# A two-layer diffusion backbone: one store form for the turned heads, query loads in 2 KB runs, rows of maxima from two queues, softmax sums in four column tiles

## The reference

```
z = h @ w_in; q_a, kv_a, k_rope, gq, gk, gv = split(z)
q  = (rms_norm(q_a, g_q_a) @ w_q_b)     # 8 heads of 64 + 32 (the 32 are rotated)
kv = (rms_norm(kv_a, g_kv_a) @ w_kv_b)  # 8 heads: 64 of key, 64 of value
gq, gk = rms_norm per head, rotated     # 8 query heads, 2 key heads of 64
o = concat(softmax(q_mla @ k_mla * scale) @ v_mla, softmax(gq @ gk * scale) @ gv)
x = layer_norm(ALPHA * x + gate * (o @ w_o)); then a two-level mixture of 32 experts
```

## Time and profile before

| | |
|---|---|
| median of 3 runs | 3547.01 us (3544.86 to 3549.27) |
| the profiled execution's own time | 3557.03 us |
| its span, first to last instruction | 3555.3 us |
| mean granted TensorE clock | 0.952 |
| TensorE matmul busy | 3211.8 us, 90% |
| VectorE busy | 2629.5 us, 74% |
| ScalarE busy | 1783.9 us, 50% |
| GpSimd busy | 1399.5 us, 39% |
| attention of layer 0 | about 385 to 940 us of the span |
| attention of layer 1 | about 2145 to 2659 us of the span |

### The profile page before, as it was taken

One profiled execution on the slowest core, in us unless ns is written; L12 is line 12 of the kernel. 1 busy time (PEld: TensorE's weight loads), 2 busy tenths in 40 slices (PEclk: granted clock), 3 DMA queues, 4 the chain that ended last, 5 costly groups with the idle time before them and its releaser, 6 DMA issues. The chain is left out here.

```text
span 3555.3 us, 44667 instructions
## 1 busy us (share of the span) xinstructions
PE 3211.8 (90%) x14764; PEld 2296.7 (65%) x14764; DVE 2629.5 (74%) x2481; ACT 1783.9 (50%) x2050; POOL 1399.5 (39%) x1103
## 2 busy tenths in 40 slices
PE   6999599998896999999959986999989699999995
PEld 3777455544484788888847764555447578888882
DVE  2444466677687899999967765777868799999995
ACT  2333233333410788888844432333432188888883
POOL 2111011121211777777732210111112278888882
PEclk9999699999997999999979997999999799999997
DMA  7665722221253989779953536222216489899965
GB/s 271 246 237 188 203 62 66 68 63 51 102 217 157 335 313 380 286 290 385 347 199 126 175 123 183 73 54 54 63 34 229 188 298 378 304 371 347 333 236 209
DMA packets 285993, 732.61 MB, mean 206 GB/s; under 512 B 65265, under 2 KB 174353, under 8 KB 234537
## 3 DMA queue, kind: packets, MB, share of 16 engines
q0 software_dynamic: 111056, 502.86, 38.3%
q1 hardware_dynamic: 157368, 175.09, 16.0%
q10 hardware_dynamic: 17440, 53.10, 4.1%
HBM read 723.65 MB, written 122.40 MB: 238 GB/s over the span
## 5 line engine op out<-in xcount | busy, mean ns | idle before, releaser
L2260 DVE TENSOR_TENSOR ex_wl<-ex_back,ex_wh 128x2048 fp32r<-128x2048 f32 x288 | 652.8, 2293 | 94.0 <-ACT ex_wh L2174 94.0
L1300 ACT ACTIVATE at_pt<-at_st 128x1024 f32<-128x1024 f32 (+1 forms) x336 | 336.6, 1004 | 561.9 <-PE at_st L1235 560.8
L2174 ACT ACTIVATE ex_wh<-ex_back 128x2048 fp32r<-128x2048 f32 x288 | 551.4, 1920 | 30.5 <-PE ex_vp L2105 17.2
L1353 DVE TENSOR_REDUCE at_nm<-at_sc 128x1 f32<-128x1280 f32 (+1 forms) x276 | 378.4, 1371 | 218.8 <-PE at_sc L1200 216.0
L1367 DVE TENSOR_TENSOR at_acc<-at_acc,at_pt 128x1024 f32<-128x1024 f32 x256 | 321.7, 1257 | 95.4 <-ACT at_pt L1300 93.2
L2260 DVE TENSOR_TENSOR ex_wl<-ex_front,ex_wh 128x2048 fp32r<-128x2048 f32 x144 | 324.0, 2290 | 12.5 <-ACT ex_wh L2174 12.1
L1249 PE MATMUL at_op<-at_pt,at_va 128*64 128x512 f32 (+1 forms) x1344 | 321.3, 607 | 0.2
L2174 ACT ACTIVATE ex_wh<-ex_front 128x2048 fp32r<-128x2048 f32 x144 | 275.3, 1923 | 86.2 <-SPq L2051 60.7
L2011 POOL DMA_INDIRECT ex_back<-in_w_down,piece_of x144 | 282.2, 1960 | 48.0 <-issue 43.4
L1235 PE MATMUL at_st<-at_q,at_km 96*128 96x512 f32 (+3 forms) x1008 | 267.2, 406 | 16.9 <-DMA at_q<-at_nmT 14.9
L1235 PEld LDWEIGHTS at_st<-at_q,at_km 96*128 96x128 f32 (+1 forms) x1008 | 181.4, 194 | 104.5 <-issue 53.6
(11 more groups left out here) (298 smaller groups left out, 6797.1 us busy)
## 6 DMA issues: line engine op xcount, KB each, us to landing
ad_w<-in_w_ada POOLq DMA_DIRECT2D x48, 1024.0 KB
at_q<-q_g SPq DMA_DIRECT2D x48, 256.0 KB, 4.4
k_n<-T SPq DMA_DIRECT2D x20, 512.0 KB, 3.6
q_n<-T SPq DMA_DIRECT2D x20, 512.0 KB, 4.2
q_g<-T SPq DMA_DIRECT2D x20, 512.0 KB, 3.4
at_km<-k_n SPq DMA_DIRECT2D x16, 640.0 KB, 10.5
mr_ot<-o_s SPq DMA_DIRECT2D x18, 512.0 KB, 5.5
h_s<-mr_h ACTq DMA_DIRECT2D x18, 512.0 KB, 2.7
```

The source lines that it names most:

```text
L1300: nc.scalar.activation(pt[:, j % PT, :, 0:nq], st[:, j % 2, :, 0:nq], ACT.Exp).then_inc(exp_done, 1)
L1353: nc.vector.tensor_reduce(nm[:, v % 3, s:s + 1], score_bank(A_NO[v, s])[:, 0:kb * P], AX.X, ALU.max, negate=True).then_inc(max_done, 1)
L2174: nc.scalar.activation(wh[:, q], early.raw(u, p), ACT.Copy).then_inc(hi_done, 1)
L2260: nc.vector.tensor_tensor(wl[:, q], early.raw(u, p), wh[:, q].bitcast(F32), ALU.subtract).then_inc(lo_done, 1)
```

## The change

1. The four groups of turned heads are stored in one form, `heads0` to `heads3`, each `[128, 2, 4, 1280]`: all in 512-byte runs, one store a group. Five stores a tile instead of eight.
2. Queries are loaded from there with the tokens of up to four tiles in one run of 2 KB (1 KB for a context unit) instead of 512 bytes, and lie in `q` by head, then tile. Keys are loaded as before, from the new names.
3. SP sends the rows of maxima of one head; the rows of the other are sent by ScalarE's queue, right behind the copy that made them.
4. The sums over partitions are four products of 32 columns of ones and half as many queries, except for the last unit, instead of two of 64 columns. ScalarE's copy is half as long, and one DMA instead of two sends the sums to memory.

```
-        NST = 8
+        NST = 5
...
-            def put_k(t):
-                sp.dma_start(S["k_n"][:, :, :, bass.ds(t * P, P)], T[0][:, :, :, :].bitcast(F32)).then_inc(q_stored, 16)
-
-            def put_q(t):
-                sp.dma_start(S["q_n"][bass.ds(t, 1)].rearrange("a p x h n -> p (a x) h n"), T[1][:, :, :, :].bitcast(F32)).then_inc(q_stored, 16)
...
+            def put(t, g):
+                sp.dma_start(S[f"heads{g}"][:, :, :, bass.ds(t * P, P)].rearrange("p x j n -> p (x j) n"),
+                             T[g][:, :, :, :].rearrange("p x j n -> p (x j) n").bitcast(F32)).then_inc(q_stored, 16)
...
-        q = sb("q", [P, QR, 2, 4, 2, P], F32R)
+        q = sb("q", [P, QR, 2, 2, 4, P], F32R)
...
-            eng.dma_start(dst.bitcast(F32), src.rearrange("a (h d) n -> d a h n", h=2)).then_inc(q_loaded[s][x], 16)
+            eng.dma_start(dst[:, :, 0:na, :].rearrange("p h a n -> p h (a n)").bitcast(F32),
+                          src.rearrange("(h d) n -> d h n", h=2)).then_inc(q_loaded[s][x], 16)
...
+        def set_row(eng, v, h):
+            pair, t0, na, kb, nq = place(v)
+            at, x = (QK, 0) if pair < G0 else (HD, 1)
+            eng.wait_ge(nm_out, T_NO[v] + 1)
+            for a in range(na):
+                eng.dma_start(q[at:at + 1, v % QR, x, h, a, :].bitcast(F32),
+                              nmT[2 * a + h:2 * a + h + 1, T_NO[v] % 2, :].bitcast(F32)).then_inc(row_set[v % QR], 16)
...
-                for h in range(2):
-                    ins = nc.tensor.matmul(op[VD * h:VD * h + VD, 0:nq], C["ones"][:, 0:VD], acc[:, u % 2, h, 0:nq], start=True, stop=True)
+                if u == len(U) - 1:
+                    for h in range(2):
+                        ins = nc.tensor.matmul(op[VD * h:VD * h + VD, 0:nq], C["ones"][:, 0:VD], acc[:, u % 2, h, 0:nq], start=True, stop=True)
+                else:
+                    for part in range(4):
+                        ins = nc.tensor.matmul(op[QB * part:QB * part + QB, 0:nq // 2], C["ones"][:, 0:QB],
+                                               acc[:, u % 2, part // 2, (part % 2) * nq // 2:(part % 2 + 1) * nq // 2], start=True, stop=True)
...
                 nc.scalar.activation(nmT[0:2 * na, n % 2, :], sc[0:2 * na, 1280:1408], ACT.Copy).then_inc(nm_out, 1)
+                set_row(act, v, 1)
...
-                for h in range(2):
-                    pool.dma_start(S["den_s"][s:s + 1, h * nq:(h + 1) * nq], den[VD * h:VD * h + 1, s, 0:nq]).then_inc(den_kept, 16)
-                pool.wait_ge(den_kept, 32 * (u + 1))
+                pool.dma_start(S["den_s"][s, 0:2 * nq].rearrange("(j n) -> j n", j=4),
+                               den[0:3 * QB + 1:QB, s, 0:nq // 2]).then_inc(den_kept, 16)
+                pool.wait_ge(den_kept, 16 * (u + 1))
```

More of the change, by code:

```diff
@@ L313, in _ @@
                 load_rope(t)
[L314 to L317, removed]
+                for g in range(4):
+                    put(t - 1, g)
                 put_v(t - 1)
@@ L327, in _ @@
             put_v(t)
[L328 to L335, removed]
+            for g in range(4):
+                sp.wait_ge(lo_done, 4 * t + g + 2)
+                put(t, g)
             sp.wait_ge(q_stored, 16 * NST * NT + 1)
@@ L977, in attention @@
     PT, QR, RC = 8, 5, 32
+    QB = P // 4
     SC = [(0, 512), (512, 1024), (1024, 1280)]
@@ L1104, in load_q @@
                     return
-                src, dst = S["q_g"][t0:t0 + na, :, part, pair - G0, :], q[part * HD:(part + 1) * HD, s, x, 0:na]
-            eng.dma_start(dst.bitcast(F32), src.rearrange("a (h d) n -> d a h n", h=2)).then_inc(q_loaded[s][x], 16)
+                src, dst = S["heads3"][:, part, pair - G0, tokens], q[part * HD:(part + 1) * HD, s, x]
+            eng.dma_start(dst[:, :, 0:na, :].rearrange("p h a n -> p h (a n)").bitcast(F32),
+                          src.rearrange("(h d) n -> d h n", h=2)).then_inc(q_loaded[s][x], 16)
         def load_k(eng, pair, x, part):
             if part == 0:
-                src, dst = S["k_n"][:, x, pair, :].rearrange("(h d) n -> d h n", h=2), km[0:NOPE, pair % 2, x]
+                src, dst = S["heads0"][:, x, pair, :].rearrange("(h d) n -> d h n", h=2), km[0:NOPE, pair % 2, x]
             else:
-                src, dst = S["k_r"][:, x, :].unsqueeze(1).to_broadcast([ROPE, 2, NT * P]), km[NOPE:QK, pair % 2, x]
+                src, dst = S["heads2"][0:ROPE, x, 3, :].unsqueeze(1).to_broadcast([ROPE, 2, NT * P]), km[NOPE:QK, pair % 2, x]
             eng.dma_start(dst.bitcast(F32), src).then_inc(k_loaded[pair % 2][x], 16)
+        def set_row(eng, v, h):
[5 more added lines that the diff above has]
+                              nmT[2 * a + h:2 * a + h + 1, T_NO[v] % 2, :].bitcast(F32)).then_inc(row_set[v % QR], 16)
         @block.sync
         def _(sp):
[L1118 to L1124, removed]
             def store(u):
@@ L1138, in _ @@
             for v in early:
-                set_row(v)
+                set_row(sp, v, 0)
             for x in range(2):
@@ L1228, in scores @@
                         K = km[:, pair % 2, :, h, keys]
-                        passes = [(K[0:QK + 1, 0], q[0:QK + 1, s, 0, 0:na, h, :]), (K[0:QK, 0], q[0:QK, s, 1, 0:na, h, :]),
-                                  (K[0:QK, 1], q[0:QK, s, 0, 0:na, h, :])]
+                        passes = [(K[0:QK + 1, 0], q[0:QK + 1, s, 0, h, 0:na, :]), (K[0:QK, 0], q[0:QK, s, 1, h, 0:na, :]),
+                                  (K[0:QK, 1], q[0:QK, s, 0, h, 0:na, :])]
                     else:
                         kv = (pair - G0) // 2
-                        passes = [(kg[:, kv, keys], q[:, s, 0, 0:na, h, :]), (kl[0:HD + 1, kv, keys], q[0:HD + 1, s, 1, 0:na, h, :])]
+                        passes = [(kg[:, kv, keys], q[:, s, 0, h, 0:na, :]), (kl[0:HD + 1, kv, keys], q[0:HD + 1, s, 1, h, 0:na, :])]
                     for m, (kk, qq) in enumerate(passes):
@@ L1403, in _ @@
             pool.dma_start(va[:, :, :], S["v_s"].rearrange("(t p) n -> p t n", p=P)).then_inc(v_loaded, 16)
-            gk = [S["k_g"][:, x, :].rearrange("(h d) n -> d h n", h=H_KV) for x in range(2)]
+            gk = [S["heads2"][:, x, 2, :].rearrange("(h d) n -> d h n", h=H_KV) for x in range(2)]
             for half in range(2):
@@ L2475, in backbone @@
     dram("ada", [2, DEPTH * 6 * D])
[L2476 to L2481, removed]
+    for g in range(4):
+        dram(f"heads{g}", [P, 2, 4, NT * P])
     dram("v_s", [NT * P, (H_MLA + H_KV) * VD])
```

24 lines of the change are left out of this document (9 added, 15 removed).

## The result

The changed kernel takes 3567.06 us (median of 7 runs, 3561.65 to 3583.01), the kernel before 3547.47 (7 runs, 3543.06 to 3550.39). The ratio is 1.0062, 95% interval 1.0044 to 1.0080: 22 us slower, 16 to 28 by the interval. The forecast was 3538.8 within 3523 to 3557, with 0.17 on slower. The profiled execution took 3567.06, its span is 3565.3 and its clock 0.948.

A forecast was written before the change was run, and what follows sets the result against it. Attention was taken as bound by TensorE, in GQA units only just. Terms -14 +12.8 -4.6 -5.0 +2.8 -1.0 -2.4 +3.2 gave -8.2 us, 3538.8 us for the median, range 3523 to 3557.

The forecast's parts named there:

- Rows issued by ScalarE: Unit hand-overs: ScalarE's four DMAs, 0.59 us each, delay the exponential and then VectorE's maximum; +12.8 us, bounds 0 and +22.
- In MLA units ... the delay is covered.: MLA hand-overs: scores take longer, TensorE comes later for the maximum, so no cost; without that cover 0.75 us each.
- 0.75 for each of 11 such hand-overs.: GQA hand-overs: TensorE loses 0.6 to 0.7 us, the next maximum can add 0.35; taken as 8.3 us in all.
- The rival that names this place: Slower: ScalarE's issuing, from 0.7 us an issue or a falling clock, holds up GQA units; +11, 3558 us; chance 0.17.
- The clock: GQA units: the slower hand-over gives TensorE two more stretches at lower clock; +3.2 us, bounds 0 and +16.
- Waits for rows: Units of layer 0: SP's last row leaves 2.5 us sooner, ending TensorE's waits; -4.6 us, bounds 0 and -5.4.
- The starts: Both starts of attention: two queues issue the last row 2.5 us earlier; -5.0 us for both layers, bounds 0 and -12.5.
- The sums: Sums in four column tiles: a latent unit takes TensorE 0.52 us for 1.00; -14 us, bounds -15.2 and -10.
- The inverse: Layer 0: one DMA instead of two brings sums forward 0.8 us at three waits; -2.4 us, bounds 0 and -8.
- Stores of one form: End of projections: 512-byte runs store slower, delaying attention's first load 1.4 us a layer; +2.8 us, bounds -4 and +4.5.
- Inside the loop the same wait is covered by TensorE's products: Projection loop: the values' copy waiting for the stores of the tile before costs nothing there.
- Loads in 2 KB runs: Query loads ahead of attention's first product go faster; -1.0 us for both layers, bounds 0 and -3.8.

The follow-up runs named there:

- run 6: Changed kernel with one added wait, holding GpSimd's product of a latent unit until VectorE's addition in the next unit: 3556.11 us, ratio 1.0012 to the kernel before.
- run 5: Changed kernel with ScalarE issuing its four rows two exponentials later, in a gap of its timeline: 3533.35 us, ratio 0.9946 to the kernel before.
- run 10: Changed kernel with ScalarE's four rows issued two exponentials later, the same kernel measured a second time: 3534.84 us, ratio 0.9945 to the kernel before.
- run 4: Kernel before with only the one store form of turned heads and the 2 KB loads of queries: 3554.56 us, ratio 1.0013.
- run 2: Kernel before with only the sums in four column tiles and their one DMA to memory: 3541.55 us, ratio 0.9981.
- runs 1 and 7: 1: changed kernel, all rows from SP, 3542.98 us; 7: kernel before with column-tile sums and rows on two queues only at attention's starts, 3535.85 us.

## Why the prediction was wrong

**Rows issued by ScalarE** is the step that failed. Its mechanism was right, and the price of an issue too: 0.61 us in the middle of 144, for the 0.59 taken. Two links behind it were wrong.
- *"In MLA units ... the delay is covered."* By the delay alone it nearly is: 0.1 us a unit in run 6. But the late exponential puts VectorE's addition beside GpSimd's product, which made it up to 1.1 us longer, ahead of the maximum; so an MLA unit of layer 1 lost 0.7 to 1.1. I had counted what stands behind the delayed instruction on its engine, and not what it now meets on the others.
- *"0.75 for each of 11 such hand-overs."* A GQA hand-over lost 1.15 without the collision and 2.2 with it. I had the maximum begin at 2516.0; it began 3.5 us late and not 2.2.

By the ratios the place alone cost 41 us (1.0062 against the 0.9946 of run 5, with both intervals 33 to 49), where the term had 12.8 with an upper bound of 22; the 28 us between are nearly all of the 30 that the forecast is off. In the profiles it is 18.2 us in layer 1 and 14.5 in layer 0 from first to last sums, beside run 10, whose mean clock there is within 0.01 of the changed kernel's. (Beside run 5, which had no stretch of lower clock in layer 1, it would be 24.6 there.) Of the 18.2 us the MLA units have 6.3. The rival that names this place had the right sign, a price too low (3558) and the wrong condition: it was to decide from 0.7 us an issue, or from a falling clock. The issue was 0.61. **The clock**, +3.2, is not seen: over the same stretches its mean is 0.98 in layer 0 and 0.99 in layer 1, before and with the change.

**Waits for rows**, -4.6: 5.4 us of waits went, as forecast, but the size owes something to the one profile: in the four other runs in which SP issued all rows of the units the same wait came to 3.6 (run 4), 1.5 (run 2) and 1.2 us (runs 1 and 7). **The starts**, -5.0: right in mechanism and, with 4.8 in the mean of the profiles, in size; in the changed kernel itself it is 4.3 (6.44 for 8.99 us, and 3.85 for 5.60).

**The sums**, -14: the work was nearly right, 0.57 us for the 0.52 taken and 15.0 us in all, but not what passes on. A GQA unit passes on only 0.3, and the time fell by 6.7 us (2.5 to 10.7) on the old form and by 11.7 on the new. **The inverse**, -2.4: not seen; VectorE waited 9.3 us for sums in layer 0 before and 9.5 with the sums and their single DMA alone.

**Stores of one form**, +2.8: 1.8 of it is seen at the tails, with 0.9 a layer for 1.4. (Behind the store of the values four stores take the place of seven, not of six as said with the change.) What failed is the sentence *"Inside the loop the same wait is covered by TensorE's products"*. In the second tile of layer 0, beside the loads of the modulation's weights, it was not: in run 5 the store that ScalarE waits for took 17.2 us to land, and TensorE stood 4.83. **Loads in 2 KB runs**, -1.0: nothing, the lower bound.

Open is why the split in the units comes out at 10 us, why the sums bring 7 to 12 us and not 15, and why in some executions the store of the second tile lands so late.

## What to carry to other kernels

DMAs issued by a compute engine are instructions of that engine: put them where its timeline shows a gap, not where their data becomes ready. Moving the four issues of a unit by two exponentials turned 22 us lost into 19 gained. When something is delayed, look at all engines for what it will now run beside, and for how late it may come: here a maximum 1.2 to 1.5 us late cost at most 0.2 in a GQA unit, 2.5 cost 1.15 and 3.5 cost 2.2. A wait should count its own transfer and not the last of five: here that hid a wait of 10 us which came in one profiled run and not in the next, though its removal brought no more than the intervals of the medians.

## What the runs showed of the hardware

VectorE's additions and GpSimd's product exclude each other. In layer 1 of the profiled runs 112 to 114 of the 128 additions of 128 x 1024 had no product beside them and took 1.21 to 1.23 us. Those that began while a product ran grew by the rest of the product, less 0.14: rest 0.44 us, 1.52; 0.67, 1.75; 0.95, 2.03; 1.24, 2.33. Where the addition was first it took its 1.22, and the product up to 2.3 instead of 1.27. Maxima, which read one operand from PSUM, stayed at 1.48 beside it. The Trainium skill has this: "SBUF — State Buffer", section "SBUF: two separate sides", says that the port pair shared by VectorE and GpSimd is an exclusive lock that the first one holds for its whole instruction, and that a VectorE operation with two SBUF inputs takes it. The trace agrees, in both directions.
